# RWKV levels on all four quarters of TensorE, staggered by groups of two blocks, with the next pair's key product among them

## What is computed

```python
def step(S, inp):
    r_t, w_t, k_t, v_t, kk_t, a_t = inp
    sa = jnp.einsum('bhij,bhj->bhi', S, -kk_t)
    S = (S * w_t[:, :, None, :] + sa[..., None] * (kk_t * a_t)[:, :, None, :]
         + v_t[..., None] * k_t[:, :, None, :])
    return S, jnp.einsum('bhij,bhj->bhi', S, r_t)
s_fin, y = lax.scan(step, s0.astype(f32), xs)
```

## Time and profile before

| what | us |
|---|---|
| median of 3 runs | 3896.39 |
| lowest, highest | 3895.34, 3896.74 |
| the profiled execution | 3899.51 |
| its span | 3897.7 |
| PE, DVE, ACT, POOL busy in the span | 2913.7, 2733.3, 1467.5, 1422.9 |

### The profile page before, as it was taken

The page is one execution under the profiler, slowest core; times in us unless marked ns, Lnnn a source line. Parts: engine busy times, 40 slices in busy tenths (PEclk is TensorE's granted clock), DMA queues, the critical chain, the costliest instruction groups (busy, mean ns, idle before and its releaser), DMA issues.

```text
span 3897.7 us, 56328 instructions
## 1 busy us (share of the span) xinstructions
PE 2913.7 (75%) x20248; PEld 1415.2 (36%) x20248; DVE 2733.3 (70%) x6400; ACT 1467.5 (38%) x4472; POOL 1422.9 (37%) x1272
## 2 busy tenths in 40 slices
PE   5999999777666656878878667888686666666665
PEld 3787777543222212433324222444242222221211
DVE  5565566367666667787787767888877777777775
ACT  1333333024333334444444434444434333333333
POOL 0011111034444444444344444333345444444442
PEclk8999999788777878989889888999898787777867
DMA  2101010289999999999999999999999999999996
GB/s 76 38 26 31 25 43 19 77 334 426 427 426 426 426 427 426 414 391 406 416 419 421 426 426 425 408 365 371 419 400 426 426 425 427 427 426 425 426 427 285
DMA packets 229929, 1313.43 MB, mean 337 GB/s; under 512 B 58768, under 2 KB 61968, under 8 KB 81808
## 3 DMA queue, kind: packets, MB, share of 16 engines
q0 software_dynamic: 165888, 1208.03, 74.0%
q1 hardware_dynamic: 63760, 101.79, 7.4%
HBM read 1303.88 MB, written 5.86 MB: 336 GB/s over the span
## 4 chain that ended last, share of the span: by engine, by line
DMA 37%; PE 19%; DVE 17%; ACT 3%; issue 3%; DVEq 1%; ACTq 1%; POOL 1%; POOLq 0%
DMA arena<-in_uv,arena 36%; DVE arena L1756 9%; PE psum L1328 8%; PE psum L1290 4%; PE psum L1380 3%; PE psum L1410 2%; DVE arena L1845 1%; ACT wbuf L1546 1%; ACT arena L1541 1%; PE psum L1400 1%; POOL arena L1270 1%; DVE arena L1684 1%; DVE arena L1819 1%; DVE level L1710 0%; DVE level L1708 0%
## 5 line engine op out<-in xcount | busy, mean ns | idle before, releaser
L1328 PE MATMUL psum<-arena,wbuf 64*64 64x512 f32 (+1 forms) x8704 | 1450.8, 739 | 862.2 <-ACT wbuf L1546 843.6
L1270 POOL DMA_INDIRECT arena<-in_uv,arena x1152 | 1342.7, 1166 | 1774.9 <-PE psum L1328 1576.2
L1756 DVE SCALAR_TENSOR_TENSOR arena<-arena 128x1024 f32<-128x1024 f32 x1152 | 1396.4, 1223 | 576.6 <-DMA arena<-in_uv,arena 562.0
L1328 PEld LDWEIGHTS psum<-arena,wbuf 64*64 64x64 f32 (+1 forms) x8704 | 337.3, 155 | 1750.7 <-ACT wbuf L1546 1356.7
L1537 ACT ACTIVATE arena<-arena 128x2 f32<-128x2 f32 x576 | 117.5, 204 | 1658.7 <-DVE arena L1756 1657.3
L1546 ACT ACTIVATE wbuf<-cst,arena 128x64 f32<-128x64 f32 x1152 | 338.9, 341 | 41.1 <-issue 1.8
L1290 PE MATMUL psum<-arena,wbuf 128*128 128x256 f32 (+1 forms) x1024 | 317.4, 459 | 8.4 <-DVE arena L1767 5.8
L1541 ACT ACTIVATE arena<-arena 128x1 f32<-128x1 f32 x1152 | 277.7, 288 | 40.8 <-issue 1.3
L1290 PEld LDWEIGHTS psum<-arena,wbuf 128*128 128x128 f32 x1024 | 206.3, 212 | 178.2 <-issue 138.1
L406 PE MATMUL psum<-arena,wbuf 128*128 128x288 f32 x768 | 211.0, 418 | 4.9 <-ACT arena L686 3.9
L1013 POOL COPY x<-arena 128x256 f32<-128x256 f32 x8 | 3.2, 398 | 465.2 <-DVE x L862 465.2
(11 more groups left out here) (275 smaller groups left out, 3266.8 us busy)
## 6 DMA issues: line engine op xcount, KB each, us to landing
wbuf<-in_w_q SPq DMA_DIRECT2D x64, 576.0 KB, 12.0
arena<-in_w_pw SPq DMA_DIRECT2D x48, 512.0 KB, 11.6
arena<-in_uv,arena POOLq DMA_INDIRECT x1152, 20.0
wbuf<-in_w_rkv SPq DMA_DIRECT2D x24, 512.0 KB, 3.8
wbuf<-in_w_o SPq DMA_DIRECT2D x8, 512.0 KB, 3.7
arena<-in_w_o SPq DMA_DIRECT2D x8, 512.0 KB, 8.1
x<-in_x SPq DMA_DIRECT2D x1, 2304.0 KB, 8.2
arena<-in_state SPq DMA_DIRECT2D x16, 128.0 KB, 3.0
```

The source lines that it names most:

```text
L1270: pool.indirect_dma_start(ring[:, g % RING, :], None, I["uv"][p // 2], bass.IndirectOffsetOnAxis(ap=idx[:, s % 4, j:j + 1], axis=0)).then_ ...
L1328: last = pe.matmul(ps[e * HD:(e + 1) * HD, 2 * (u % 2) + a if u < NB else 4, :], diag[t, g % DIAGS, :], ring[t, g % RING, D + e * 512:D + ...
L1756: stt(out=row, in0=row, scalar=1.0, in1=tok[p % 2][:, UNITS[p % 2].index(u), :], op0=ALU.mult, op1=ALU.mult, accum_out=dots[:, g % COLS:g ...
```

## The change

The levels no longer go head by head but by groups g of two blocks, both heads in each group. Head 0 stays on the two diagonal quarters, head 1 has its halves swapped: its input half j goes to output partitions of half 1 - j (`of_head(j ^ e)`), so four products in a row lie on the four quarters. Turn, y and dXT of one head and group now share one bank (columns 0, `Y_AT` = 128, `D_AT` = 256). ScalarE copies turned blocks and y of both heads with one activation a group (`XY[g]`, 384 columns from two banks; 512 in the corner level). VectorE's add and the POOL coefficients are by group too, with as many elements and as many instructions as before. The token transposes use banks 6, 7, 6.

`front` begins with the first half of the key product k0, then wa0, wa1, k1, and the rest as before. Its eight k0 steps are taken inside the levels, between the second y and the first dXT: `fill((0, 0, 1, 1, 2, 2, 2)[l])`. `rows_R(0)` stands ahead of wa0. The fills further down are smaller:

| place | before | after |
|---|---|---|
| between Y and S of block 0 and s_RT | 6, 3, 3, 5, 3, 3, 4 | 3, 3, 3, 3, 2, 1 |
| between s_RT and mean | 3, 3, 3, 4, 4 | 1, 3, 3, 2, 4, 4 |
| left over after mean | 4 | 8 |

ScalarE's key copies of half 0 move from behind U of block 0 to ahead of R of block 0, and the sigmoids to behind it. The buffers co and XY[1] lie in another dead region. In the first pass's own front the same new order holds.

```diff
             def front(n):
+                pe.wait_ge(wl[0], n * 16 + 16)
+                if n:
+                    pe.wait_ge(dve_s.sem, dve_s.value(f"gramRK0.{n - 1}"))
+                yield from project(n, xm[1], 0, 0, "k")
                 pe.wait_ge(low_loaded, n * 16 + 16)
                 for h in range(2):
-                    if h:
-                        pe.wait_ge(act_s.sem, act_s.value(f"a0.{n}"))
-                    elif n:
-                        pe.wait_ge(act_s.sem, act_s.value(f"tok_k.{n - 1}"))
-                        pe.wait_ge(dve_s.sem, dve_s.value(f"XT{LEVELS - 1}_0.{n - 1}"))
+                    pe.wait_ge(act_s.sem, act_s.value(f"{('k0', 'a0')[h]}.{n}"))
...
                 for l in range(1, LEVELS):
-                    for e in range(2):
+                    corner = l == LEVELS - 1
+                    for g in range(2):
                         if l > 1:
-                            pe.wait_ge(dve_s.sem, dve_s.value(f"XT{l - 1}_{e}.{i}"))
+                            pe.wait_ge(dve_s.sem, dve_s.value(f"XT{l - 1}_{g}.{i}"))
...
+                        for b in range(2):
+                            for e in range(2):
+                                for j in range(1 if corner else 2):
+                                    last = pe.matmul(ps[of_head(j ^ e), 4 * g + e, b * HD:(b + 1) * HD], XTd[of_head(j), e, 2 * g + b, :],
+                                                     K.ident2[of_head(j)], start=True, stop=True)
+                        if not corner:
+                            pe.wait_ge(pool_s.sem, pool_s.value(f"co{l}_{g}.{i}"))
+                        for b in range(2):
+                            for e in range(2):
+                                for j in range(0 if corner else 2):
+                                    out = ps[of_head(j ^ e), 4 * g + e, Y_AT + b * HD // 2:Y_AT + (b + 1) * HD // 2]
+                                    last = pe.matmul(packed(out, l), co[l % 2][g][of_head(j), e, b, :], later(XTd[of_head(j), e, 2 * g + b, :], l),
                                                      start=True, stop=True)
...
                     if l == 3:
                         pe.wait_ge(act_s.sem, act_s.value(f"tok_v.{i}"))
-                        tokens(i, "tok_k", kt, 3)
+                        tokens(i, "tok_k", kt, 6)
+                    fill((0, 0, 1, 1, 2, 2, 2)[l])
+                    for g in range(2):
+                        pe.wait_ge(act_s.sem, act_s.value(f"y{l}_{g}.{i}"))
+                        for b in range(2):
+                            for e in range(2):
+                                for j in range(1 if corner else 2):
+                                    q, width = of_head(j ^ e), HD if corner else HD // 2
+                                    last = pe.matmul(ps[of_head(j), 4 * g + e, D_AT + b * width:D_AT + (b + 1) * width],
+                                                     XY[g][q, e, b * HD:(b + 1) * HD],
+                                                     XY[g][q, 1 - e if corner else e, Y_AT + b * width:Y_AT + (b + 1) * width], start=True, stop=True)
...
-                fill(1)
                 pe.wait_ge(act_s.sem, act_s.value(f"tok_k.{i}"))
                 pe.wait_ge(dve_s.sem, dve_s.value(f"XT{LEVELS - 1}_1.{i}"))
                 rows_R(0)
+                fill(1)
...
                 for l in range(1, LEVELS):
+                    for g in range(2):
+                        act.wait_ge(pe_s.sem, pe_s.value(f"y{l}_{g}.{i}"))
+                        f = slice(0, P + HD if l < LEVELS - 1 else 2 * P)
+                        act.activation(XY[g][:, :, f], ps[:, 4 * g:4 * g + 2, f], ACT.Copy).then_inc(act_s.at(f"y{l}_{g}.{i}"), 1)
...
                     act.wait_ge(prm_loaded, n * 16 + 16)
+                    key(n, 0)
+                rows_R(0)
+                if more:
                     decay_and_rate(n, 0)
-                rows_R(0)
```

More of the change, by code:

```diff
@@ L279, in wkv @@
     Q0 = Region(K.arena, dead_at)
-    co = [[Q0.cut(NB, HD) for _ in range(2)] for _ in range(2)]
-    y1 = [Q0.cut(NB * HD) for _ in range(2)]
+    co = [[Q0.cut(2, NB // 2, HD) for _ in range(2)] for _ in range(2)]
+    XY.append(Q0.cut(2, 2 * P))
+    assert Q0.at <= dead_at + 3 * N
     Q2 = Region(K.arena, l_at)
@@ L343, in later @@
     def later(view, l):
+        if len(view.shape) == 3:
+            return view.rearrange("p e (g two r) -> p e g two r", two=2, r=2 ** l)[:, :, :, 1, :]
         return view.rearrange("p (g two r) -> p g two r", two=2, r=2 ** l)[:, :, 1, :]
     def packed(view, l):
+        if len(view.shape) == 3:
+            return view.rearrange("p e (g r) -> p e g r", r=2 ** l)
         return view.rearrange("p (g r) -> p g r", r=2 ** l)
@@ L503, in _ @@
                 for l in range(1, LEVELS):
-                    for e in range(2):
+                    corner = l == LEVELS - 1
+                    for g in range(2):
                         if l > 1:
-                            pe.wait_ge(dve_s.sem, dve_s.value(f"XT{l - 1}_{e}.{i}"))
-                        elif e == 0:
+                            pe.wait_ge(dve_s.sem, dve_s.value(f"XT{l - 1}_{g}.{i}"))
+                        elif g == 0:
                             pe.wait_ge(dve_s.sem, dve_s.value(f"gramG1.{i}"))
[L509 to L520, removed]
@@ L525, in _ @@
-                        last.then_inc(pe_s.at(f"y{l}_{e}.{i}"), 1)
+                                if corner:
+                                    last = pe.matmul(ps[of_head(e), 4 * g + 1 - e, Y_AT + b * HD:Y_AT + (b + 1) * HD], L_low[HD:P, e, 2 * g + b, :],
+                                                     XTd[HD:P, e, 2 * g + b, :], start=True, stop=True)
+                        last.then_inc(pe_s.at(f"y{l}_{g}.{i}"), 1)
                     if l == 1:
-                        pe.wait_ge(dve_s.sem, dve_s.value(f"gramRK0.{i}"))
@@ L528, in _ @@
-                        tokens(i, "tok_v", v_s, 3)
+                        pe.wait_ge(dve_s.sem, dve_s.value(f"gramRB1.{i}"))
+                        tokens(i, "tok_v", v_s, 6)
                     if l == 2:
@@ L533, in _ @@
                         pe.wait_ge(act_s.sem, act_s.value(f"tok_v.{i}"))
-                        tokens(i, "tok_k", kt, 3)
[L535 to L548, removed]
+                        tokens(i, "tok_k", kt, 6)
[9 more added lines that the diff above has]
+                                                     XY[g][q, 1 - e if corner else e, Y_AT + b * width:Y_AT + (b + 1) * width], start=True, stop=True)
+                        last.then_inc(pe_s.at(f"dXT{l}_{g}.{i}"), 1)
                 def rows_R(b):
@@ L618, in _ @@
                 rows_Y_S(0)
-                fill(6)
+                fill(3)
                 sample_y(1)
@@ L652, in _ @@
                 last.then_inc(pe_s.at(f"s_U.{i}"), 1)
-                fill(3)
+                fill(2)
                 rows_Y_S(3)
@@ L715, in _ @@
             act.wait_ge(prm_loaded, 16)
+            key(0, 0)
             for h in range(2):
                 decay_and_rate(0, h)
-            for h in range(2):
-                key(0, h)
+            key(0, 1)
             for part in range(3):
```

69 lines of the change are left out of this document (29 added, 40 removed).

## The result

The changed kernel takes 3855.99 us (median of 4, 3853.11 to 3860.17) against 3896.56 for the kernel before on the same chip: ratio 0.989, 95% interval 0.9878 to 0.9902. That is 40.6 us less. The forecast was 23 less (3873, range 3859 to 3890): right in sign, too small by 17, and the result is outside the range by 3.

What follows compares the result with a forecast made beforehand. TensorE's issue was taken to bound a pass. Seven passes -25.6, last pass -3.5, start +4 and clock +2 sum to -23.1 us, from median 3896.4 to 3873; range 3859 to 3890.

Steps and rivals of the forecast that it cites:

- The price of a record: TensorE in the levels: every record on four quarters costs 19.5 ns, 0.31 us per group of 16.
- (A): Rival, levels: 32-column records no faster on four quarters, 27.5 ns for y and dXT; +15.6 us, 3889; chance 0.10.
- (B): Rival, levels: records have a floor whatever the quarters, 27.5 ns for all; +26 us, 3899; chance 0.03.
- The clock: Passes: +0.3 us a pass, +2 in all, since TensorE stands before R0 and before the second decay product.
- Rival (D): After the idle before R0 the clock falls and stays at half; +42 us, 3915; chance 0.06.
- Level 6 to S of block 0: Stretch from level 6's start to S of block 0, with R moved ahead of the first decay product: +0.9 us a pass.
- that chain moves as it is: First to second decay and rate product: 3.08 us, including waits for a table load and two sigmoids, stays unchanged.
- S of block 0 to the samples' rows: Between S of block 0 and the sample rows: 27 steps become 15 at 0.50 us each, -6.0 us a pass.
- Rival (C): State chain shows through: one microsecond of bare waiting in each of three blocks a pass; +21 us, 3894; chance 0.06.
- The tail: After the sample rows: 21 steps become 25, +2.0 us, less VectorE slack, so +1.75 us a pass.
- The start: First pass: the key product now leads and its second half comes later; +4 us once, from +2 to +6.
- the last pass: Last pass, without fill steps: its five levels take 13.2 us against 16.7, -3.5 us.

Runs made afterwards that it cites:

- the levels alone: New levels only, with key-product order, fills and ScalarE's order as in the kernel before and no steps in the levels: 3875.79 us, ratio 0.994 to the kernel before.
- two quarters again: Changed kernel with head 1 back on the two diagonal quarters in levels 1 to 5, all else kept: 3910.04 us, ratio 1.0026 to the kernel before.
- each turn twice: Changed kernel with each turn product of levels 1 to 5 issued twice to the same output: 3886.56 us, ratio 0.9972 to the kernel before.

## Why the prediction was wrong

**The price of a record: the step that failed, mis-sized.** "I take 19.5 ns for all" is 17.5 for 64 columns and 13 for 32. The nearest four-quarter row was a bad guide. Its 19.5 is the mean of 80 records that are spread unevenly: by the code of `small_gram`, each of the two quarters of half 1 gets 24 of them and each of the others 16, and 24 rounds of 58 ns are 1.40 of the 1.56 us; the rest is the longer first step and the change to the next shape. In the levels each quarter gets a quarter of the records. The lower bound of the forecast, half of the two-quarter 27.5 (13.8), had that right. With 0.28 and 0.21 us a group the forecast's own formula gives 2.49, 2.99, 2.99, 3.05, 3.05 us; measured were mostly 2.68, 2.98, 2.98, 3.08, 3.08, with single levels up to 0.4 longer. Level 1 is held by VectorE's masks: they end at 340.70, and the add comes only behind them, at 340.76, though its dXT started at 340.15. All five levels are 1.5 us a pass under the forecast, 10 in seven, and 0.4 of the last pass's extra 1.6. Rivals (A) and (B), which have 32-column records no faster than 27.5 ns, are out. So is, for tiles in four quarters, the floor that the Trainium skill states (TensorE: Matmul & The Clock Gate, "Wait — 56ns, not 53.3ns?"): here starts on different quarters are 7 ns apart.

**The clock: wrong in sign.** The forecast added 0.3 us a pass because TensorE stands longer before R0. It stands 1.15 instead of 0.99 us, and yet the falls vanished, -0.5 instead of +0.3: 5.7 us. The step went by the idle alone and forgot what stands beside it. The clock goes with the two full-array steps in level 6: moving them to levels 4 and 5 brings seven falls, and in the levels alone two dummies in their place remove all but one. With levels of 20 us in all (two quarters again) they weren't enough. The price of a fall was misread too: the windows of the earlier trace rows are not whole periods. From grams to grams the pass of the first window took 78.6 us against 76.7, 2.0 more and not 1.05; the two others that fell took 0.7 and 0.9 more. Rival (D) is real as a mechanism: it is what the levels alone and the moved steps suffer from.

**Level 6 to S of block 0:** +0.37 measured, +0.9 forecast. R0 came 0.68 us earlier after level 6's start (3.67 for 4.35), where the forecast's working gives 0.55. But from the first decay product to the second are 2.65 us instead of 3.08, where "that chain moves as it is" kept 3.08. The table load stands 0.40 us behind the product's start, before that product has ended, and stood 0.84 behind it before; here after (product at 358.03) and before (product at 450.16):

```profile
358.44 1.28 ACT L687 ACT_TABLE_LOAD   x1
...
451.00 1.28 ACT L685 ACT_TABLE_LOAD   x1 [2.56 <-PE psum L424]
```

Why it can start sooner was not tried.

**Grams to level 1:** no change forecast, -0.5 measured, shown above to be GpSimd's product beside VectorE's adds. The diff had it (`gram_L1` for `gram_L{e}`), and the trace had adds of unequal length; the prediction passed over both.

**S of block 0 to the samples' rows:** -5.89 for -6.0. Right, and with it the reading that the state chain is covered. Rival (C) is out.

**The tail:** +2.69 for +1.75. Of the missing 0.94, 0.75 is a new wait, as the run with Y copied first shows: with more steps left over after the mean, the last step of v0 stands directly before the mean, and ScalarE's list has its copy ahead of Y's. The prediction counted steps and did not walk ScalarE's list there.

**The start** +3.5 for +4, **the last pass** -5.1 for -3.5: besides the levels (0.4), grams to level 1 (0.5) and level 6 to S of block 0 (0.4) are shorter there too.

In seven passes the errors are -10 (levels), -6 (clock), -3.5 (adds), -4 (level 6) and +7 (tail). The tail hid part of the others; without that luck the forecast would have been further off. The range took in only the rate and two us of clock, and was 3 us short.

## What to carry to other kernels

Spreading small tiles over all quarters nearly halved their issue here, also at 32 columns, and without it the rest of the change gains nothing. A mean per record read off one row holds for another only if the records are spread as evenly: count the records of the busiest quarter. Where TensorE must wait at the end of a sparse stretch, a full-array product in front of the wait, useful or not, can be worth more than its time, as the clock then fell less often here. After moving steps in one engine's hand-written list, walk the lists of the others past the new places: two of the surprises (ScalarE's copy order, GpSimd's later start) stood there.

## What the runs showed of the hardware

- 64x64 tiles with 32 columns in fp32: 27.5 ns a record on two quarters, 13 on four; with 64 columns 32.5 and 17.5. Both come from rounds of 58 ns a record on each quarter; the grams kept 19.5 because two of the quarters have 24 of the 80 records each.
- With the faster levels TensorE shows idle that no semaphore explains: 5.3 us in seven passes of the levels alone (waits of up to 1.0 us), 3.5 with each turn twice, none listed before, after, or with two quarters. Levels of one kernel then differ by up to 1.4 us from pass to pass. What causes it was not tried.
- Two unused 128x128x288 products in level 6 of the levels alone: falls of the clock in one pass of seven instead of six, and 18 us less.
- Two VectorE adds of 128x256 in fp32 between SBUF tensors took 0.42 us each alone and 0.46 and 0.88 beside a GpSimd product.
